# Second attention: row sums from a column of ones, and VectorE's work of a unit in another order

## The reference, cut

```python
s = q @ k.T + bias            # per head, 256 positions, causal
p = softmax(s)                # exp(s - max), divided by its row sum
o = p @ v                     # 64 columns per head
out = sum over the branches of sigmoid(gate) * o
```

## Time and profile before

| | us |
|---|---|
| median of 3 executions | 1597.65 |
| lowest and highest | 1597.32, 1603.59 |
| profiled execution | 1600.37 |
| its span in the trace | 1598.6 |
| TensorE busy | 1533.4 (96%) |
| VectorE busy | 1030.2 (64%) |
| ScalarE busy | 797.7 (50%) |

### The profile page before, as it was taken

How to read it: one execution, slowest core, us unless ns; L and a number is a source line. 1 busy time by engine, 2 the same in 40 slices (tenths; PEclk the granted TensorE clock), 3 DMA queues, 4 the chain that set the end, 5 groups by cost and what they waited for, 6 DMA issues and landing times.

```text
span 1598.6 us, 25010 instructions
## 1 busy us (share of the span) xinstructions
PE 1533.4 (96%) x10255; PEld 1381.4 (86%) x10255; DVE 1030.2 (64%) x1704; ACT 797.7 (50%) x1437; POOL 223.3 (14%) x189
## 2 busy tenths in 40 slices
PE   8999999999999999989999999999989799999999
PEld 6899889799987889989889987788877699989887
DVE  5764586787756675578678765555755586666643
ACT  5555454366643455445456653453446664455532
POOL 2300032211102120032031100012010050100000
PEclk9989999999999999999999999999999799999999
DMA  8623255355565533255355555555212144645453
GB/s 310 246 102 99 91 211 185 136 197 183 185 217 189 189 122 118 81 198 185 109 197 180 182 200 178 186 197 185 90 46 76 53 158 157 206 163 184 159 190 123
DMA packets 40353, 258.19 MB, mean 162 GB/s; under 512 B 4512, under 2 KB 5168, under 8 KB 14000
## 3 DMA queue, kind: packets, MB, share of 16 engines
q1 hardware_dynamic: 35600, 238.44, 42.8%
q0 software_dynamic: 2272, 12.57, 2.1%
q10 hardware_dynamic: 2368, 5.58, 0.9%
HBM read 254.98 MB, written 1.07 MB: 160 GB/s over the span
## 4 chain that ended last, share of the span: by engine, by line
PE 73%; DVE 13%; ACT 8%; issue 4%; DMA 2%; POOL 1%; ACTq 0%; POOLq 0%; DVEq 0%; SPq 0%
PE ps L492 65%; DVE lows L1557 5%; ACT wh L1037 3%; PE ps L602 3%; PE ps L683 1%; ACT S L1460 1%; DVE ar L2093 1%; PE ps L704 1%; DMA raw<-d_wst 1%; ACT arR L1538 1%; DVE S L2274 1%; DVE S L2155 1%; DVE xTr L1576 1%; PE ps L722 1%; PE ps L721 0%
## 5 line engine op out<-in xcount | busy, mean ns | idle before, releaser
L1557 DVE TENSOR_TENSOR lows<-raw,wh 128x1024 fp32r<-128x1024 f32 (+3 forms) x473 | 544.9, 1171 | 249.8 <-ACT wh L1037 247.2
L492 PE MATMUL ps<-xTr,wh 128*128 128x256 f32 (+2 forms) x3472 | 633.8, 285 | 3.4 <-DVE S L1924 1.6
L492 PEld LDWEIGHTS ps<-xTr,wh 128*128 128x128 f32 (+2 forms) x3472 | 537.9, 190 | 8.8 <-DVE S L1924 3.0
L1037 ACT CAST wh<-raw 128x1024 fp32r<-128x1024 f32 (+3 forms) x473 | 455.2, 989 | 176.6 <-DMA raw<-d_wst 131.4
L492 PE MATMUL ps<-xTr,lows 128*128 128x256 f32 (+1 forms) x1736 | 491.3, 283 | 0.0
L492 PEld LDWEIGHTS ps<-xTr,lows 128*128 128x128 f32 (+1 forms) x1736 | 330.0, 190 | 0.0
L492 PE MATMUL ps<-wh,arR 128*128 128x512 f32 x928 | 298.2, 399 | 7.4 <-DVE ar L1746 4.0
L492 PEld LDWEIGHTS ps<-wh,arR 128*128 128x128 f32 x928 | 175.1, 189 | 52.7 <-DVE ar L1746 5.7
L492 PE MATMUL ps<-lows,arR 128*128 128x512 f32 x464 | 184.1, 397 | 0.0
L492 PE MATMUL ps<-wh,xTr 128*128 128x512 f32 x480 | 153.3, 397 | 16.7 <-DVE xTr L1576 13.1
L492 PE MATMUL ps<-arR,wh 128*128 128x256 f32 (+1 forms) x832 | 148.7, 281 | 0.0
(11 more groups left out here) (259 smaller groups left out, 1514.7 us busy)
## 6 DMA issues: line engine op xcount, KB each, us to landing
raw<-d_wst SPq DMA_DIRECT2D x196, 1024.0 KB, 4.9
raw<-d_wst SPq DMA_DIRECT2D x24, 512.0 KB, 3.5
raw<-d_wst SPq DMA_DIRECT2D x12, 896.0 KB, 4.5
raw<-d_wst SPq DMA_DIRECT2D x8, 672.0 KB, 4.6
ar<-d_lnp POOLq DMA_DIRECT2D x5, 1024.0 KB, 5.2
raw<-d_wst SPq DMA_DIRECT2D x8, 441.0 KB, 3.5
ar<-d_par POOLq DMA_DIRECT2D x2, 1192.0 KB, 9.6
ar<-d_scr POOLq DMA_DIRECT2D x1, 2048.0 KB, 9.2
```

The lines of the kernel that those rows point to most:

```text
L492: op = e.matmul(out, s, m, start=start and i == 0, stop=stop and i == len(pairs) - 1)
L1037: e.copy(high_of(m), raw_of(m)).then_inc(*high.done(m))
L1557: e.tensor_tensor(low_of(m), raw_of(m), high_of(m).bitcast(F32), ALU.subtract).then_inc(*low.done(m))
```

## The change

Values and row sums: `vb` gets a 65th column for each head, set to 1.0 by GpSimd, so that each pv product gives the row sum in its own 65th column; the exponentials no longer write sums. The reciprocal of the sum and the product with the gates move from `maxima` to `finish`, behind the pv product. On VectorE a unit now is: maxima of un, copy of un - 1, output of un - 2, and the two filling items that stood in unit un - 1. The last three items and the outputs of units 6 and 7 follow at the end. TensorE's and ScalarE's order stays. The buffer `arena` grows by 16 columns.

```diff
@@ buffers @@
-ARENA = 25360
+ARENA = 25376
...
-        vb = arena(1024).rearrange("p (i c) -> p i c", i=2)
+        vb = arena(1040).rearrange("p (i h d) -> p i h d", i=2, d=65)
@@ TensorE, finish @@
+                    w.wait_ge(pool, "ones")
...
-                            v = br * 256 + h * 64
-                            op = e.matmul(b[:, h * 64:(h + 1) * 64], PTv[:, hold + h, k, :], vb[:, k, v:v + 64],
+                            op = e.matmul(b[:, h * 65:(h + 1) * 65], PTv[:, hold + h, k, :], vb[:, k, 4 * br + h, :],
@@ ScalarE @@
-                    e.copy(vb[:, i, j * 256:(j + 1) * 256], b[:, 256:512]).then_inc(*act.done("vb", j, i))
+                    e.copy(vb[:, i, 4 * j:4 * j + 4, 0:64], b[:, 256:512].rearrange("p (h d) -> p h d", d=64)).then_inc(*act.done("vb", j, i))
...
-                        op = e.activation(Sv[:, hold + h, 0:nk], Sv[:, hold + h, 0:nk], ACT.Exp, bias=nb[:, h:h + 1], scale=1.0,
-                                          accum_out=su[:, h:h + 1])
-                        op.then_inc(*act.done("exp2", i, un))
+                        e.activation(Sv[:, hold + h, 0:nk], Sv[:, hold + h, 0:nk], ACT.Exp, bias=nb[:, h:h + 1],
+                                     scale=1.0).then_inc(*act.done("exp2", i, un))
@@ VectorE, maxima @@
-                    go = 16 * (br + 1) + 4 * hq
-                    w.wait_ge(act, "exp2", i, un)
-                    e.reciprocal(ri, su).then_inc(*vec.done("ri0", i, un))
-                    w.wait_ge(vec, "ri0", i, un)
-                    e.tensor_tensor(ri, ri, ng[:, i, go:go + 4], ALU.mult).then_inc(*vec.done("ri2", i, un))
@@ VectorE, finish @@
+                    go = 16 * (un // 4 + 1) + 4 * (un % 4)
+                    o = M["pv2", i, un][:, 0:260].rearrange("p (h d) -> p h d", d=65)
                     w.wait_ge(cross, "pv2", i, un)
+                    e.reciprocal(ri, o[:, :, 64]).then_inc(*vec.done("ri0", i, un))
+                    w.wait_ge(vec, "ri0", i, un)
+                    e.tensor_tensor(ri, ri, ng[:, i, go:go + 4], ALU.mult).then_inc(*vec.done("ri2", i, un))
...
-                                    M["pv2", i, un][:, 0:256].rearrange("p (h d) -> p h d", d=64),
+                                    o[:, :, 0:64],
@@ VectorE, the units @@
                 for un in range(8):
+                    maxima(un)
                     if un:
                         probs_copied(un - 1)
-                    maxima(un)
-                    lru_next(2)
+                    if un > 1:
+                        finish(un - 2)
                     if un:
-                        finish(un - 1)
+                        lru_next(2)
                 probs_copied(7)
-                lru_next(1)
+                finish(6)
+                lru_next(3)
                 finish(7)
@@ GpSimd @@
+            e.memset(vb[:, :, :, 64:65], 1.0).then_inc(*pool.done("ones"))
```

## The result

The changed kernel takes 1581.32 us (median of 4 executions, 1579.54 to 1585.33), the kernel before beside it 1599.87 (median of 4, 1597.32 to 1603.59): ratio 0.9886, 95% interval [0.9855, 0.9916], some 18 us faster. The prediction of 1579.1 us was 2.2 low, with the sign right and the time inside its range. The profiled execution of the changed kernel took 1585.33 us (span 1583.5), the longest of its four.

The account below looks back on a forecast made before the run. TensorE waits in both attention blocks while VectorE and ScalarE take turns. Block 0's -9.15 and block 1's -9.45 sum to -18.6 us, applied to the median 1597.65: 1579.1 us, range 1574 to 1587.

Parts of the forecast that it names:

- The rings: VectorE and ScalarE take turns while TensorE waits; opening this gives -9.55 us (block 0) and -6.34 us (block 1).
- The thinnest place: Convolution units of i = 0: VectorE's low half is ready 0.2 us before TensorE's second feature needs it, so no wait.
- rival B: VectorE becomes the bound in i = 0's convolution units: +1.2 to +8 us, 1580.3 to 1587 us; chance 0.13.
- VectorE's unit is the sum of its rows: Convolution units of i = 0: VectorE's steps sum to 7.7 us, hardly under TensorE's 7.74 us.
- The tail: End of i = 1: last pv product, behind a chain of decay steps, starts 10.65 us after the last scores start, -3.5 us.
- Reciprocal and multiplication behind the last product: End of each attention block: these steps now follow the last pv product instead of preceding it, +0.4 us each.
- The estimate of 0.065 us: Reciprocal moved from SBUF to PSUM would cost 0.065 us more, 0.13 us on the two tails.
- Between the blocks: From the transposes of y of i = 0 to the first scores of i = 1: forecast difference 0.
- The other terms taken for nothing: 65th column (between 0 and 3.4 us), strided copy of v (0 to 0.2 us each), ones on GpSimd: taken as 0.
- rival E: Filling products wait for pv banks freed a unit later by VectorE's output: slower, 1603.7 us; chance 0.04.

Follow-up runs that it names:

- the first three runs: Edits of the changed kernel: VectorE's old order, 1598.72 us; new order with the wait for exponentials, 1607.03; new order with exponentials' sums, no column or wait, 1581.6.
- the fourth: Changed kernel with VectorE's share of the filling work made in its own unit, behind the output of un - 2: 1589.18 us, ratio 0.9926.

## Why the prediction came out right

**The rings.** Both were read rightly. i = 1 came out as forecast (T of unit 1 to T7: -6.34, all units 6.42). i = 0 gave -9.21 for -9.55. That VectorE's order decides, and not the exponentials' sums as such, the forecast had in its sums but didn't say; the first three runs show it, and the fourth shows that without the share's delay 5.8 of the 9.21 us of i = 0 are gone.

**The thinnest place.** VectorE's unit was summed to 7.7 us with 0.2 of cover for the low half. The sum lacked one term: 0.42 us in the units in which GpSimd's addition overlaps the share. With it VectorE's unit measured 7.99 us (the rest came out at 7.57, a little under the sum) and two of TensorE's units 7.85 and 7.99: rival B in small, +0.34 in the block. The step that failed is "VectorE's unit is the sum of its rows": each row was taken from a place where GpSimd was idle or VectorE was reading scores from PSUM.

**The tail.** The chain was named rightly (decay steps ahead of the last copy), its end was 0.83 us late: 11.48 for 10.65. VectorE's product for the second decay step ended at T + 9.24 (1251.28 + 0.76 - 1242.80) where I had T + 8.4. The same term is missing: L2072 is 0.95 instead of 0.41 and L2076 0.76 instead of 0.42, both beside GpSimd's additions; 0.54 + 0.34 = 0.88. With the additions elsewhere both take 0.42 (the run with the output last).

**Reciprocal and multiplication behind the last product.** +0.41 and +0.45 for +0.4 each; the earlier trace rows have 1.41 us of idle ahead of the transposes of y, now 1.82. The PSUM read costs nothing that shows: the reciprocal from PSUM takes 0.17 us and the next instruction starts 0.21 after it (1157.21 to 1157.42), the one from SBUF took 0.18 and 0.21 (1191.33 to 1191.54 in the kernel before). The estimate of 0.065 us from the Trainium skill (Perfetto Trace Analysis, Optimizing Scalar/DVE Operations) isn't borne out for this shape (128x4).

**Between the blocks.** Taken at 0 and not named among the rivals: +1.76. The longer idle time was in my sum as +0.4, but whether clock could be lost behind it wasn't asked. The same question was asked for the tail, where the answer (half clock behind the gap, 3.67 us for the sixteen records) was right. Without this term and the two above, the trace would have come within 0.1 us of the forecast 18.6.

**The other terms taken for nothing** were nothing that shows: eight records with 65 columns take 1.00 us, as those with 64 did, and the strided copy and the ones aren't seen on the path. The bank of the pv product (rival E) had its cover; only with the output still later it began to bite.

## What to carry over

Where an engine waits for another engine's work of the same unit, taking away one wait only uncovers the next instruction that needs something from the same producer. Here it helped only once what VectorE asks for was a unit old. So judge such a change by the ring as a whole, and don't expect its parts to gain one by one. Where a cover is 0.2 us, look at what the neighbour engines do in exactly these microseconds, and at whether a wait that gets longer has costly work behind it.

## What the hardware showed that I had not expected

GpSimd's addition on SBUF (128x256, two inputs) takes 0.72 us by itself or beside VectorE's maxima, whose scores come from PSUM, but 1.51 and 1.64 us where VectorE makes a low half; VectorE's next instruction then takes 0.83 for 0.41, or 0.95 for 0.41. The records look like turns, not like sharing: the addition starts at 1158.12, the low half ends at 1159.03, the addition 0.60 us later, and only then does the long L2087 end. By the Trainium skill (SBUF — State Buffer, SBUF: two separate sides) VectorE with two SBUF inputs and a GpSimd instruction that reads SBUF take an exclusive lock on a shared pair of ports, and the other blocks. This case's trace agrees in the main: the low half reads two tensors of SBUF and began first (1157.95), and the addition was held up. It isn't exact: the addition ends 0.60 us behind the low half, not the 0.72 that it takes by itself. L2087 reads only one tensor, so the sentence on two inputs doesn't speak of it; that it is long is what the trace shows. The change moves the output, and so the addition, from beside the maxima to beside a low half, and I hadn't weighed that.

Behind a stretch in which TensorE had hardly waited (55.96 of 56 us busy), 1.82 us of idle were followed by 1.2 GHz; behind one in which it had waited for 4 us in all (58.45 of 62.5 us busy), the same idle was not. Two idle products in the gap kept the clock at 1.00. I have no run that says why.
